# A gate projection as seven half-size block products instead of eight, woven into an attention stage

## The reference, cut to what matters

```python
h = rms_norm(x, attn_norm[l])
proj = jnp.einsum('bsd,dc->bsc', h, w_in[l])
(fq, fk, fv, ff, cu, cb, cc, mq, mk, mv, mi, mf, mo, sq, sk, sv,
 gates) = jnp.split(proj, split_points, axis=-1)
...
g = jax.nn.sigmoid(gates.reshape(B, S, N_BRANCH, D_MODEL))
merged = (g[:, :, 0] * jnp.einsum('bsw,wd->bsd', y_fox, w_fox_out[l])
          + g[:, :, 1] * jnp.einsum('bsw,wd->bsd', y_conv, w_conv_out[l])
          + g[:, :, 2] * jnp.einsum('bsw,wd->bsd', y_mlstm, w_mlstm_out[l])
          + g[:, :, 3] * jnp.einsum('bsw,wd->bsd', y_swa, w_swa_out[l]))
```

## Time and profile before

| | us |
|---|---|
| median of 3 runs (3227.25 to 3241.75) | 3228.24 |
| the profiled execution | 3227.97 |
| its span, first to last instruction | 3226.2 |
| PE busy in it | 3039.4 (94%) |
| DVE busy | 1820.3 (56%) |
| ACT busy | 1548.8 (48%) |
| GpSimd busy | 383.7 (12%) |
| gated attention with the gates in it | 1755 to 2352, 597 long |
| row projection before it | about 1478 to 1749 |

### The profile page before, as it was taken

The page is one execution under the profiler, slowest core; times in us unless marked ns, Lnnn a source line. Parts: engine busy times, 40 slices in busy tenths (PEclk is TensorE's granted clock), DMA queues, the critical chain, the costliest instruction groups (busy, mean ns, idle before and its releaser), DMA issues. The chain is left out here.

```text
span 3226.2 us, 40247 instructions
## 1 busy us (share of the span) xinstructions
PE 3039.4 (94%) x15105; PEld 2503.5 (78%) x15105; DVE 1820.3 (56%) x2658; ACT 1548.8 (48%) x2454; POOL 383.7 (12%) x349
## 2 busy tenths in 40 slices
PE   7998999898969999969998999999999999999999
PEld 6766999686857888858777877788877778888887
DVE  4336888424678888873321222342266576666685
ACT  4225777533458888853522333333453342222443
POOL 0001110000233333220000000000000032222000
PEclk9999999899979999979999999999999999999999
DMA  3334221312168888661233222243265233334653
GB/s 112 90 122 118 60 60 31 118 34 86 72 258 295 287 303 290 234 211 53 79 107 108 61 71 79 66 134 95 69 217 162 72 92 98 101 114 125 224 159 114
DMA packets 252834, 417.75 MB, mean 129 GB/s; under 512 B 45143, under 2 KB 159902, under 8 KB 240354
## 3 DMA queue, kind: packets, MB, share of 16 engines
q1 hardware_dynamic: 228002, 369.77, 35.6%
q10 hardware_dynamic: 9088, 28.58, 2.3%
q0 software_dynamic: 15552, 16.82, 1.8%
HBM read 372.11 MB, written 106.39 MB: 148 GB/s over the span
## 5 line engine op out<-in xcount | busy, mean ns | idle before, releaser
L2856 DVE TENSOR_TENSOR moe_wgu_low<-moe_raw,moe_wgu_high 128x2048 fp32r<-128x2048 f32 x92 | 206.7, 2289 | 45.6 <-ACT moe_wgu_high L2792 39.1
L224 PE MATMUL ga_gate<-second_h_high,ga_ws_high 128*128 128x512 f32 x512 | 222.4, 434 | 6.6 <-DVE ga_ws_low L4009 6.6
L226 PE MATMUL ga_gate<-second_h_high,ga_ws_low 128*128 128x512 f32 x512 | 204.5, 399 | 0.0
L225 PE MATMUL ga_gate<-second_h_low,ga_ws_high 128*128 128x512 f32 x512 | 203.9, 398 | 0.0
L2792 ACT ACTIVATE moe_wgu_high<-moe_raw 128x2048 fp32r<-128x2048 f32 x92 | 171.2, 1909 | 20.2 <-ACT moe_y L2801 20.2
L224 PE MATMUL up_bank<-second_h_high,up_w_high 128*128 128x512 f32 x352 | 139.2, 396 | 8.8 <-DVE up_w_low L3487 7.3
L3939 ACT ACTIVATE ga_row<-ga_turned 128x256 f32<-128x256 f32 (+4 forms) x96 | 44.6, 465 | 211.8 <-PE ga_turned L3852 211.6
L224 PE MATMUL pr_acc<-second_h_high,pr_ws_high 128*128 128x512 f32 x336 | 137.7, 410 | 5.8 <-DVE pr_stage L3228 5.8
L225 PE MATMUL up_bank<-second_h_low,up_w_high 128*128 128x512 f32 x352 | 138.8, 394 | 0.0
L226 PE MATMUL up_bank<-second_h_high,up_w_low 128*128 128x512 f32 x352 | 138.4, 393 | 0.0
L2961 POOL DMA_INDIRECT moe_rows<-scratch_ffn_rows,slot_of_block x47 | 110.7, 2356 | 226.2 <-PE moe_turned L2745 159.0
(11 more groups left out here) (650 smaller groups left out, 8491.1 us busy)
## 6 DMA issues: line engine op xcount, KB each, us to landing
moe_raw<-in_w_expert_gate_dram SPq DMA_DIRECT2D x32, 1024.0 KB, 4.9
moe_raw<-in_w_expert_up_dram SPq DMA_DIRECT2D x32, 1024.0 KB, 6.9
moe_raw_down<-in_w_expert_down_dram SPq DMA_DIRECT2D x32, 1024.0 KB, 5.6
scratch_expert_rows<-moe_y ACTq DMA_DIRECT2D x46, 512.0 KB, 4.2
scratch_hidden<-X SPq DMA_DIRECT2D x77, 256.0 KB, 2.1
down_rows<-scratch_hidden SPq DMA_DIRECT2D x73, 256.0 KB, 3.1
scratch_gates<-ga_stage SPq DMA_DIRECT2D x64, 256.0 KB, 4.1
mb_spare<-scratch_gates SPq DMA_DIRECT2D x32, 512.0 KB, 3.6
```

Source lines behind the costliest of these rows:

```text
L224: nc.tensor.matmul(out, w[0], x[0], start=start, stop=False)
L225: nc.tensor.matmul(out, w[0], x[1], start=False, stop=False)
L226: return nc.tensor.matmul(out, w[1], x[0], start=False, stop=stop)
L2856: nc.vector.tensor_tensor(wgu[i % 2][1][:, :, m, :], raw[(2 * i + m) % RAW][:].rearrange("p (c n) -> p c n", n=FF), wgu[i % 2][0][:, :, m, ...
```

## The change

The gate product is computed by Strassen's scheme in Winograd's form, as a 2 x 2 block product of half-size blocks. Two groups of 128 gate columns that lie 16 groups apart make a pair (16 pairs); with the two halves of the 1024-long contraction they give four weight quarters A11, A12, A21, A22 of 128x512. The tokens give four blocks B (contraction half x token half). Seven products of 4 chunks x 3 matmuls replace eight of the same size.

The products are ordered in two parts, because of the token blocks: first, for each of the 16 pairs, A11 B11, S2 T2, A12 B21, S1 T1; then, for each pair again, A22 T4, S3 T3, S4 B22. T1, T2, T4 are sums and differences of token blocks. They are computed in the row projection stage: 15 DVE instructions of 128x2048 elements (`block_sum`). Two results stay in `swa_y` and `fox_y`, three go to memory (`keep_block`, 1 MB each) and are loaded back at the turn from the first part to the second (`load_block`). When a block is due, `swap_high` (ACT) and `swap_low` (DVE) split it into the place in `HT` that its products read: two blocks before step 0, three at steps 73, 74 and 75.

The weight sums S1, S2 (first part) and S3, S4 (second part) are GpSimd instructions of 128x512 (`combine`), 2 x 16 + 3 x 16 = 80 of them, each waited for by GpSimd itself. Every product has its own weight split: 112 high parts of 128x512 on ACT and 112 low parts on DVE, in a ring of three. SP loads the quarters (256 KB each) for the next pair after the low part that frees them; the weights are read twice, once for each part.

A result block is a sum of several products. Of the products, A11 B11 leaves its bank by an ACT copy; all others leave through additions on DVE that read the bank and a stage tile, 96 products and a second addition for each S3 T3, 112 additions. What is not complete after the first part goes to memory as a partial and is loaded again in the second (`load_partial`); there are 96 stores and 32 partial loads of 256 KB.

The steps: product 0 stands before step 0, product q stands in step q + int((q - 0.7) x 19 / 111), so 19 of the steps 0 to 129 have none. The additions for a product come first in DVE's program in the next step, in front of the shift; the split for product q + 3 comes after it. The two memsets of GpSimd stand between the sums.

The diff, cut to its core:

```diff
+            def keep_block(m, sums):
+                sp.wait_ge(k.block_sums, sums)
+                sp.dma_start(kept_blocks[m], sum_tile).then_inc(k.blocks_kept, 16)
...
+                if j in (11, 15, 19):
+                    keep_block((11, 15, 19).index(j), {11: 7, 15: 10, 19: 11}[j])
+            for n in range(2):
+                sp.wait_ge(lows, N - 1 + n)
+                sp.dma_start(raw[n][:, :, :], w_view[:, :, C_GATES + n * HALF:C_GATES + n * HALF + P]).then_inc(k.first_gate_in, 16)
...
+            block_ops = [(sum_tile, h12, h11, ALU.subtract), (sum_tile, sum_tile, l12, ALU.add), (sum_tile, sum_tile, l11, ALU.subtract),
+                         (sum_tile, h22, sum_tile, ALU.subtract), (sum_tile, sum_tile, l22, ALU.add),
+                         (sum_tile, h21, sum_tile, ALU.subtract), (sum_tile, sum_tile, l21, ALU.add),
+                         (sum_tile, h22, h12, ALU.subtract), (sum_tile, sum_tile, l22, ALU.add), (sum_tile, sum_tile, l12, ALU.subtract),
+                         (sum_tile, h22, l22, ALU.add),
+                         (late_tile, h12, h11, ALU.subtract), (late_tile, late_tile, l12, ALU.add),
+                         (late_tile, late_tile, l11, ALU.subtract), (sum_tile, sum_tile, late_tile, ALU.subtract)]
+            op_at = {**{2 + i: (i,) for i in range(7)}, 11: (7,), 12: (8,), 13: (9,), 16: (10,), 19: (11,), 20: (12,), 21: (13, 14)}
+
+            def block_sum(i):
+                if i:
+                    dve.wait_ge(k.block_sums, i)
+                for first, stored_blocks in ((7, 1), (10, 2), (14, 3)):
+                    if i == first:
+                        dve.wait_ge(k.blocks_kept, 16 * stored_blocks)
+                out, a, b, op = block_ops[i]
+                v.tensor_tensor(out, a, b, op).then_inc(k.block_sums, 1)
...
+        weights = [pair(k, f"ga_ws{b}", [P, PART, P], ctx) for b in range(RING)]
+        stage = [k.sb(f"ga_stage{b}", [P, HALF], ctx=ctx) for b in range(4)]
...
-        bounds = [PRODUCTS * i // (2 * GATE_SLOTS) for i in range(2 * GATE_SLOTS + 1)]
...
+        first_four, last_three = (A11_B11, S2_T2, A12_B21, S1_T1), (A22_T4, S3_T3, S4_B22)
+        gate_order = [(m, i) for m in range(PAIRS) for i in first_four] + [(PAIRS + p, i) for p in range(PAIRS) for i in last_three]
+        N_GATE, TURN = len(gate_order), len(first_four) * PAIRS
+        empty_steps = 130 - (N_GATE - 1)
+        step_of = [-1] + [q + int((q - 0.7) * empty_steps / (N_GATE - 1)) for q in range(1, N_GATE)]
+        product_at = {step: q for q, step in enumerate(step_of)}
+        evac_at = {step + 1: q for q, step in enumerate(step_of)}
+        split_at = {step + 1: q + RING for q, step in enumerate(step_of) if q + RING < N_GATE}
+        swap_at = {step_of[TURN - 3] + 2: 2, step_of[TURN - 2] + 2: 3, step_of[TURN - 1] + 2: 4}
...
+        weight_of = {A11_B11: A11, S2_T2: A11, A12_B21: A12, S1_T1: A21, S3_T3: A11, S4_B22: A12, A22_T4: A22}
+        block_of = {A11_B11: (lo, first_half), S2_T2: (hi, second_half), A12_B21: (hi, first_half), S1_T1: (lo, second_half),
+                    S3_T3: (hi, second_half), S4_B22: (lo, second_half), A22_T4: (lo, first_half)}
...
+        swaps = [block_of[i] for i in (S2_T2, S1_T1, A22_T4, S3_T3, S4_B22)]
+        swap_of = {S2_T2: 1, S1_T1: 2, A22_T4: 3, S3_T3: 4, S4_B22: 5}
...
+            def load_quarters(q):
+                m, i = gate_order[q]
+                free = {S2_T2: (A11, A22), A12_B21: (A12,), S1_T1: (A21,), S3_T3: (A21,), S4_B22: (A11, A12, A22)}.get(i, ())
+                if m + 1 == 2 * PAIRS or not free:
+                    return
+                sp.wait_ge(lows, q + 1)
+                for a in free:
+                    n, chunks = place[a]
+                    col = C_GATES + rows_of(m + 1, n)
+                    sp.dma_start(quarter(m + 1, a), w_view[:, chunks, col:col + P]).then_inc(quarters_in[a], 16)
...
+            def store_gate(q):
+                m, i = gate_order[q]
+                if i in (A11_B11, A22_T4):
+                    return
+                sp.wait_ge(*evacuation(q))
+                for done in (S3_T3, A22_T4) if i == S3_T3 else (i,):
+                    t = tile_for(m, done)
+                    sp.dma_start(gates_place(m, done), stage[t][:]).then_inc(out[t], 16)
+
+            def load_partial(m, i):
+                t = tile_for(m, i)
+                sp.wait_ge(out[t], stored_before(m, i))
+                source = S1_T1 if i == S4_B22 else S2_T2
+                sp.dma_start(stage[t][:], gates_place(m, source)).then_inc(k.partials_in[t], 16)
+
+            def load_partials(q):
+                m, i = gate_order[q]
+                if q == TURN - 3:
+                    load_partial(PAIRS, S4_B22)
+                if q == TURN - 1:
+                    load_partial(PAIRS, A22_T4)
+                if i == A22_T4 and m + 1 < 2 * PAIRS:
+                    load_partial(m + 1, S4_B22)
+                if i == S4_B22 and m + 1 < 2 * PAIRS:
+                    load_partial(m + 1, A22_T4)
+
+            def load_block(n):
+                c, tokens = swaps[n]
+                sp.wait_ge(gate_products, TURN - 3 + (0, 1, 3)[n - 2])
+                sp.dma_start(HT[1][:, c, tokens].bitcast(F32), kept_blocks[n - 2]).then_inc(k.blocks_in[n - 2], 16)
...
+            for q in range(RING):
+                load_quarters(q)
...
+                if s in evac_at:
+                    store_gate(evac_at[s])
+                    load_partials(evac_at[s])
+                if s + 1 in swap_at:
+                    load_block(swap_at[s + 1])
+                if s in split_at:
+                    load_quarters(split_at[s])
...
+            def combine(m, into, a, b, op, count):
+                nc.gpsimd.tensor_tensor(quarter(m, into), quarter(m, a), quarter(m, b), op).then_inc(sums_made, 1)
+                pool.wait_ge(sums_made, sums_of(m, count))
+
+            for m in range(2 * PAIRS):
+                for g in (4, 5):
+                    if m == 2 * g - 2:
+                        pool.wait_ge(products, ST * (g - 1))
+                        for tile in (q_of(g * ST), k_of(g * ST)):
+                            nc.gpsimd.memset(tile[HD:HD + 2, :], 0.0).then_inc(made, 1)
+                        pool.wait_ge(made, 4 + 2 * (g - 3))
+                for a in (A21, A22) if m < PAIRS else (A11, A21):
+                    pool.wait_ge(*quarter_in(m, a))
+                if m < PAIRS:
+                    combine(m, A21, A21, A22, ALU.add, 1)
+                    pool.wait_ge(lows, first_of(m) + 1)
+                    combine(m, A11, A21, A11, ALU.subtract, 2)
+                else:
+                    combine(m, A11, A11, A21, ALU.subtract, 1)
+                    pool.wait_ge(*quarter_in(m, A12))
+                    pool.wait_ge(*quarter_in(m, A22))
+                    combine(m, A12, A12, A11, ALU.add, 2)
+                    combine(m, A12, A12, A22, ALU.subtract, 3)
...
-            def gates(quantum):
-                for x in range(bounds[quantum], bounds[quantum + 1]):
-                    u, c = x // KD, x % KD
-                    j = u // 2
-                    if c == 0:
-                        if u % 2 == 0:
-                            pe.wait_ge(lows, j + 1)
-                        if u >= 2:
-                            pe.wait_ge(evacuated, u - 1)
-                    last = add_product(nc, gate_ps[u % 2][:], part(weights[j % 2], slice(None), c, slice(None)),
-                                       part(HT, slice(None), c, slice(u % 2 * HALF, (u % 2 + 1) * HALF)), c == 0, c == KD - 1)
-                    if c == KD - 1:
-                        last.then_inc(gate_products, 1)
-
-            for quantum in range(4):
-                gates(quantum)
+            def gates(q):
+                m, i = gate_order[q]
+                pe.wait_ge(lows, q + 1)
+                if q >= 2:
+                    pe.wait_ge(*evacuation(q - 2))
+                if m in (0, PAIRS) and i in swap_of:
+                    pe.wait_ge(k.block_lows, swap_of[i])
+                chunks, tokens = block_of[i]
+                moving = part(HT, slice(None), chunks, tokens)
+                for c in range(PART):
+                    last = add_product(nc, gate_ps[q % 2][:], part(weights[q % RING], slice(None), c, slice(None)),
+                                       part(moving, slice(None), c, slice(None)),
+                                       c == 0, c == PART - 1)
+                last.then_inc(gate_products, 1)
+
+            gates(0)
...
-                if 2 <= s < GATE_SLOTS:
-                    gates(2 * s)
-                    gates(2 * s + 1)
+                if s in product_at:
+                    gates(product_at[s])
...
+            def high_part(q):
+                m, i = gate_order[q]
+                if i in (A11_B11, A12_B21, A22_T4):
+                    act.wait_ge(*quarter_in(m, weight_of[i]))
+                else:
```

(57 more changed lines are left out.)

146 lines of the change are left out of this document (81 added, 65 removed).

## The result

The changed kernel took 3264.11 us (median of 4 runs, 3259.79 to 3270.55), the kernel before 3227.74 beside it (4 runs): 1.0109 of it, 95% interval 1.0078 to 1.0140. It is 36 us slower; the prediction said 3225, and the range ended at 3256.

What follows compares the result with a forecast made beforehand. TensorE was taken to set the gated attention stage's end. -45.3 + 15.5 + 7 + 5 + 11.9 + 3 = -2.9 us on a span of 3226.2 gave a forecast median of 3225 us, range 3196 to 3256.

Steps and rivals of the forecast that it cites:

- Partials through memory: Second part: store, reload and additions over three products take 12.25 us against PE's 12.3; 3 us charged, bounds 0 and 40.
- ring of partials: Rival, second part: store plus load of partials exceed 6.95 us, so the next score waits; 3246 us, chance 0.20.
- The change doesn't shorten the stage: Rival, gated attention: freed PE time turns wholly into waits for high and low parts; 3228 to 3235 us, chance 0.06.
- The block: Gate product: a block of 12 matmuls takes 2.83 us on PE; 16 blocks fewer save 45.3 us.
- Empty window steps: Seven window steps without a product: each idles PE 0.74 us behind ACT's copy, 5.2 us together.
- falls of the clock at empty steps: Steps without a product: idle PE lowers the granted clock; two falls taken, 7 us, from a possible none to ten.
- Turn: Token blocks swapped between the two parts: 8.5 us of landing and splits plus one clock fall, 11.9 us, bounds 4 and 20.
- Moved work: Work shifted to engines with room in the stage: DVE gains 126 us, GpSimd gets 104 us of sums.
- The block sums: Row projection: 15 DVE sums of 2.3 us fit where DVE waits for ACT; uncovered they would cost 34 us.
- Start: Start of the stage: extra weight and token-block splits before step 0's shift cost 5 us, bounds 2 and 9.
- Step 41: Lstm step without a product: a head's division stands in front of PE's additions, priced at 3.0 us.
- GpSimd holds DVE: Rival: each of 80 GpSimd sums stops a DVE instruction for 1.3 us, +104 us, 3329 us; chance 0.04.

Runs made afterwards that it cites:

- the early quarters: On the changed kernel, weight quarters A22 and A11 loaded behind S3's low part and the third sum, one product sooner: 3275.74 us, ratio 1.0163 to the kernel before.
- the version with both transfers early: On the changed kernel, weight quarters loaded one product earlier and A22's partial one pair ahead using a fifth tile, nothing left out: 3229.14 us, ratio 1.0018.
- the best version: Changed kernel with quarters and partials loaded earlier, chunks spread evenly, later block sums, shorter start, token-block splits in halves: 3213.74 us, ratio 0.9951.

## Why the prediction was wrong

**The step that failed is "Partials through memory", 3 us.** The second part cost 33.8 us against -8.2. Moving both transfers takes 42.4 of it away in the profiled executions (33.8 to -8.6), and 35 of the 39 us between forecast and result by the medians: nearly the whole miss. Three things in that step were wrong:

- It had one ring, where there are two. The quarters of A22 were judged hidden, since SP's wait "is in the ring" and three split weights stand ahead of PE. But the unsplit quarter is not three deep: A22 comes first in a pair, its tile is freed by the last product of the pair before, and ACT asks for it one step later. Issue 1.5, landing and the way to ACT made 6.4 us from S4's low part (2174.52) to A22's high part (2180.90). The median landing of all these loads in the second part is 3.5 us, under the 4.1 of the earlier trace rows, but A22's, issued third of three, has a median of 4.5 (3.9 to 5.6); issued first, as with the early quarters, it has 3.0. So mostly the lead was too short, and its place in the queue made it shorter.
- Its balance, 12.25 against 12.3 us, was that of a ring without the others in it. By itself it held: from the issue of A22's store to the landing of its load the change has 6.6 us (median of 15 pairs), under the 6.95 that the prediction gave as the limit. With the quarters early it is 8.7, and the partials set the pace, at 43.6: their loads stand behind three quarter issues on SP's queue. The rival "ring of partials" came nearest, with 3246; but its loads left out alone give nothing.
- It was charged no fall of the clock. From 1750 to 2400 us the clock's record has 95.6 us at the half level in 15 stretches, and 44.4 in 7 for the kernel before; half of the difference, 25.6 us, is lost, against 7 + 3.4 in the sum. Most of it is in the second part: from 2147 to 2384, 41.2 us against 6.8, so 17 us lost. Six of the seven falls there stand at an idle time of PE of 1.4 to 3.8 us, the seventh at one of 0.8; one of 1.5 us (2274.9) was followed by none. So of the 42 us between the two stretches above nearly half is clock, not waiting.

The sentence in "The change doesn't shorten the stage" that set three parts in flight against a chain of 8 us is the same mistake; that rival named what happened and priced it at 3235.

**Right, or nearly.** The block: steps 3 to 72 gained 18.7 where the sum has 16.3. Empty window steps: 1.84 instead of 3.85 (step 103 of the version with both transfers early), so 2.0 of the 2.83 are gained, where 0.74 of idle time had made it 2.1. The 7 us for falls of the clock at empty steps did not come: from 1758 to 2110 the change has 34.3 us at the half level, the kernel before 32.3. Turn: 10.3 against 10.0, and that is partly luck: the blocks' landing, counted as 6.5 us (it was 6.7 to 7.4), costs nothing (3263.53 without it), and the profile puts no wait of PE down to a token block's low part, as the prediction had it, but 8.0 us to DVE's `ml_y`, 6.9 of them behind two of these low parts in DVE's order. That the splits are the cost is argued from that wait; halving them gave 2.8 us of the turn's 21.7. Moved work: DVE +167 us in all (126 and 15 x 2.3 predicted, 160), GpSimd +112 (104). The block sums did not lengthen the row projection by their own time: it began 1.9 later and ended 3.9 later (1752.6), with PE waiting 3.2 us for two low parts; the weight load issued behind the first stored block took 7.2 us. The first gate matmul came 2.9 later. Start: 7.5 us at step 3, predicted 5; with the 2.9 off it is 4.6. Two counts in the prediction are off and change little: a step before had 9 or 12 gate matmuls, not 11 or 12, and 21, not 23, stood in front of the score at 1766.29.

**Step 41 and the clock.** The order of time there, and the stretch around it, in the change and then in the kernel before:

```profile
1982.67 0.66 PE L4015 MATMUL ga_turned<-vm,swa_y 128*128 128x65 f32 x2 [2.80 <-issue]
1983.13 2.87 PE L3984 MATMUL ga_scores<-X 66*128 66x512 f32 x4
```

```profile
1978.00:1990.00 12.00, 9.07 (x20) 5.92 (x21) 5.96 (x15) 3.17 (x6) 0.00 (x0) 0.58 0.50 132
1978.00:1990.00 12.00, 12.00 (x39) 8.65 (x38) 5.11 (x12) 4.54 (x9) 0.00 (x0) 0.72 0.23 67
```

PE idles 2.8 us in front of the additions, near the 3.0 of the prediction, and step 41 is 5.01 us against 7.74 before. Step 42 is 7.88 against 4.48. The two steps together are 12.9 us against 12.2: nothing of the block's 2.83 is left, and 0.7 more is lost. The kernel before had a fall here too, in step 41, behind the same 1.5 us of idle time in front of the score; its record has 6.8 us at the half level from 1978.0, that of the change 10.2 from 1980.0. Most of PE's idle time lies in it, and step 42 runs almost whole at the half level (0.58 against 0.72 over these 12 us).

**GpSimd holds DVE**, chance 0.04: 18 us of the 36 go when the sums are cut, so it is part of the cost, and not by 1.3 us at each sum (104). That it costs where DVE's order has no slack is the reading that fits; it is not shown, since with the transfers early the cut is still worth 0 or 12 us. The 18 and the 35 of the transfers overlap and cannot be added.

## What to carry to other kernels

When a product's operand is loaded, summed and split, count the lead from the freeing of the raw tile to the first instruction that reads it, not from the depth of the split ring; load first what is read first, and put loads that are late in front of others on the queue. When two waits end in one order of work, take both away in one kernel before judging either: here -3 and +12 us alone, neither clear of noise, and -39 together; with nothing left out +8 and +12 alone, and -35 together. And count in the clock: here the waits that came back in nearly every pair, 19 us in all, cost about as much again in matmuls at half speed.

## What was not expected of the hardware

- The clock's share: about 19 of 42 us (an estimate, above) between two stretches with the same matmuls. Executions of one kernel differ by it as well: 3219.4 at 0.970, 3255.0 at 0.957 (above).
- The convolution's DVE product of 128x1024 took 2.28 us beside GpSimd's sums (2182.79 above), 1.21 in a step of the version with early transfers.
- With both transfers early the DMA share of the second part rose from 0.55 to 0.68 and the median landing of the quarters only from 3.5 to 3.9 us; ACT did not wait for them.

Open are the turn, which still costs 18.9 us in the best version, and what the sums cost once the transfers are early.
